# A two-layer transformer step with seven-product multiplications: groups of 8, 8 and 6 feed-forward units, two plain chunk pairs in place of three, and the weight-block sums on GpSimd

## The chip, the core and the metric

One Trainium2 chip; the kernel runs on one of its cores. The metric is the device time of one execution in microseconds (us), the median over runs: 2202.97 us before the change (three runs, 2202.61 to 2203.21). Engines by the names in the profile: PE is TensorE's matmul, PEld its weight load, DVE is VectorE, ACT is ScalarE, POOL is GpSimd, SP starts the DMAs.

## The reference, cut to what matters

Two layers over 640 tokens (128 context, 512 latent) of width 1024. The part of a layer that the change touches is its end, the gated feed-forward with an inner width of 2816 = 22 units of 128, and the projection `h @ w_in` at its start, which is computed by the same routine.

```python
h2 = rmsnorm(x, norm2_g) * (1.0 + sc2) + sh2
a, b = jnp.split(h2 @ w_ffn_in, 2, axis=-1)
return x + g2 * ((jax.nn.silu(a) * b) @ w_ffn_out)
```

All data are float32. The kernel multiplies in a reduced format: each operand is split into a rounded high part and a remainder (low part), and a product is three matmuls: high by high, high by low, low by high.

## The kernel before, in words

**Chunks.** A chunk is 128 output rows by 640 tokens. TensorE reads a weight block of 128x128 and passes 320 tokens, so a plain chunk over a depth of 1024 is 8 x 3 x 2 = 48 matmuls of 320 columns. Chunks come in pairs; in the feed-forward the pair is one unit's `a` and `b`.

**Eight products and seven.** A plain pair is 96 matmuls (in block terms eight half-depth products). A fast pair uses seven half-depth products, P1 to P7 (a Strassen-Winograd scheme), of 12 matmuls each: 84. It needs, of the raw weights of each pair, four sums of blocks of 128x512 (`weight_sums`, numbered 1 to 4, executed in the order 1, 3, 2, 4), and of the activations four blocks of sums and differences per layer and place, made once (`turned_sums`, four of 128x1280, then a high part each by ACT in `turned_hi` and a low part by DVE in `turned_lo`; they are written to `TT` and, for number 1, over part of `H`). Sum 1 is the weight of P5, sum 3 that of P7, sum 2 that of P6, sum 4 that of P3.

**Ring.** The weights of the products, split in high (`fast_hi`, ACT) and low (`fast_lo`, DVE), stand in a ring of six slots inside `wr`. The two halves of the ring are also the two buffers for the weights of plain chunks. `HI_STEP` says after which product a slot is free again. The order of the products is written out by `ring_order`: P1 of pair 0, then for each pair P2, P6, P7, P5, P1 of the next pair, P3, P4. ACT and DVE walk through the same list (`fast_step`): at each step they take results out of PSUM (ACT those of P1, P6, P7 and P3; DVE those of P2, P5 and P4), then split the weights of a product that comes six steps later. Each engine works strictly in the order of its program.

**Banks.** A pair's P1, P6, P5 and P3 accumulate in one bank, `lp[m % 2][:, 0]`; P2 goes to `lp[0][:, 1]`, P7 and P4 to `lp[1][:, 1]`. P6 may start only when ACT has copied P1's result out (`p1_out`), P5 only when ACT has copied P6's (`u2_out`), P3 only when DVE has added P5's (`c22_out`), P4 only when ACT has copied P7's (`p7_out`).

**Groups.** The 22 feed-forward units are computed in three groups, A, B and C (8, 7 and 7). Group A begins with three plain pairs (`first_pair`, then `chunk`), and during these ACT adds the shift to the normalised rows (`raw_rows`) and ACT and DVE make the four turned blocks. Then come the fast pairs (5 in A, 7 in B, 7 in C; 6 at the layer's start, behind three plain pairs), and behind each group its part of the second product (`outward`: 8 chunks over 8, 7 and 7 units), which starts when the last products have left their banks and its weights are split (`out_first_hi`, `weight_lo`). The values that `outward` reads, `G`, are finished pair by pair (`c12_out` by ACT, a multiplication and `hidden_lo` by DVE).

**Sums before.** The four weight sums of a pair are made by DVE between its other work: 2 x 25 pairs x 4.

**Loads.** SP issues the raw weights of a pair in two parts; a slot is free again when the pair two before it has been split. The second part of an odd pair lies in `wx`, over the activations' raw rows, and for the first such load of group A SP waits until turned blocks have been read (`t_lo`).

The lines that decide where the second product's first weights may be written are these, and the change leaves them as they are:

```python
places = [i % RING for i in range(n)]
if places[-1] == 0:
    places[-1] = RING // 2
...
used = max(i for i, r in enumerate(RING_AT[g]) if r // (RING // 2) == s)
act.wait_ge(prod, OPS * pairs_before(l, g, 0) + used + 1)
```

Of the kernel before, what the change touches and what calls it, by code (L numbers as in the profile page):

```python
# [52 lines left out]
FA, FB, FC = 8, 7, 7  # L53
PLAIN = 3
# [4 lines left out]
SLOTS = (2 * PLAIN, N_GATE, KD, 2 * PLAIN, KD, 0, KD, 0, KD)  # L59
SLOT0 = [sum(SLOTS[:i]) for i in range(10)]  # L60
CHUNKS = (2 * PLAIN, 2 * N_GATE, KD, 2 * PLAIN, KD, 0, KD, 0, KD)
# [13 lines left out]
FAST = ((IN_A + IN_B) // 2 - PLAIN, FA - PLAIN, FB, FC)  # L75
FAST0 = [sum(FAST[:i]) for i in range(5)]
FIRST = (PLAIN, PLAIN, FA, FA + FB)
INNER0 = (0, PLAIN, 0, 0)
# [141 lines left out]
def build(nc, xT, ada, adb, win, wgu, wo, wff, wfa, wfb, vec, cond, fgv, cst, rope, dft, bias, ckT, cvt,  # L220
          yT, okT, ovt):
    with ExitStack() as ctx:
# [318 lines left out]
        def _(sy):  # L541
# [24 lines left out]
            def raw_pair(l, g, m):  # L566

                for part in range(2):
# [3 lines left out]
                    else:  # L572
                        before = 1 + l * PER_SLOT + SLOT0[AHEAD[g]] // 2
                        sy.wait_ge(w_lo[0 if r == 0 else 1], before)
                        if r == 3 and g <= FAST_A:
                            sy.wait_ge(t_lo, turned_set(l, g) + 3)
# [42 lines left out]
            for l in range(L):  # L619
# [83 lines left out]
                for j in range(PLAIN):  # L703
                    for s in range(2):
                        weight(l, FF_A, wff, j, s)
                for g in FF_GROUPS:
# [9 lines left out]
                    for s in range(2):  # L716
                        sy.wait_ge(op_lo, nth_op(l, g, FAST[g] - 1, (P3, P4)[s]))
# [32 lines left out]
        def _(pe):  # L750
# [45 lines left out]

            def fill(l, p, place):

                for n, k in FILL.get((p, place), ()):
# [8 lines left out]
                    else:  # L808
                        if k == KD:
# [172 lines left out]
            def fast_product(l, g, i):  # L982
# [26 lines left out]
                if which == P5:  # L1009
                    pe.wait_ge(u2_out, n + 1)  # L1010
                    if new_blocks:
                        pe.wait_ge(t_lo, turned_set(l, g) + 4)
                if which == P3:
                    pe.wait_ge(c22_out, n + 1)
                if which == P4:
                    pe.wait_ge(p7_out, n + 1)
                    if new_blocks:
                        pe.wait_ge(t_lo, turned_set(l, g) + 3)
# [19 lines left out]
            for l in range(L):  # L1038
# [68 lines left out]
                for i, (m, which) in enumerate(ORDER[FAST_IN]):  # L1107
# [6 lines left out]
                    if which == P4:  # L1114
# [18 lines left out]
                for out_of in (c11_out, c12_out, c21_out):  # L1133
                    pe.wait_ge(out_of, pairs_before(l, FAST_IN, FAST[FAST_IN]))
# [49 lines left out]
                for j in range(1, PLAIN):  # L1184
# [4 lines left out]
                for g, inner in zip(FF_GROUPS, (S_GA, S_GB, S_GC)):  # L1189
# [27 lines left out]
        def _(act):  # L1217
# [108 lines left out]

            def fast_step(l, g, i):
# [6 lines left out]
                if which == P1:  # L1334
                    if n:
                        act.wait_ge(c11_out, n)
                    if g == FAST_A and m == 0:
                        act.wait_ge(split, l * PER_SPL + SP0[S_GA] + 2)
                    act.activation(t1[:, 0:TH], A, ACT.Copy).then_inc(p1_out, 1)
# [84 lines left out]
            for l in range(L):  # L1424
# [38 lines left out]
                for o in range(RING // 2, RING):  # L1463
# [76 lines left out]
                def plain_hidden(i, s):  # L1540
# [11 lines left out]
                plain_hidden(0, 0)  # L1552
# [5 lines left out]
                act.wait_ge(lin[1], 1 + l * PER_DR + D0[FF_A] + PLAIN)  # L1558
                turned_hi(l, FAST_A, 1)
                for g in FF_GROUPS:  # L1560
# [4 lines left out]
                    for o in range(RING // 2, RING):  # L1565
# [17 lines left out]
            root(2 * L + 1)  # L1583

        @block.vector
        def _(ve):
# [254 lines left out]
            def weight_sums(l, g, m, which):  # L1841

                if m >= FAST[g]:
                    return
                n = pairs_before(l, g, m)
                a, b = raw(m, 0), raw(m, 1)
                a11, a12, a21, a22 = a[:, 0:QC], a[:, QC:2 * QC], b[:, 0:QC], b[:, QC:2 * QC]
                for s in which:
                    if s == 1:
# [430 lines left out]
```

## Time and profile before

| | |
|---|---|
| median of three runs | 2202.97 us (2202.61 to 2203.21) |
| the profiled execution | 2201.25 us, its span 2199.5 us |
| PE busy | 2137.2 us, 97% of the span |
| DVE busy | 1309.4 us, 60% |
| ACT busy | 900.8 us, 41% |
| POOL busy | 0.2 us, four small writes at the start |

A busy row of PE counts each matmul with its latency, so rows overlap; how long a matmul really takes is read from the start of one merged row to the start of the next. "Idle before" behind a row is the time in which the engine did nothing before it, and the arrow names the instruction that ended it ("issue" where the profile shows none). The chain of waits lies on PE nearly all the time.

### The profile page before, as it was taken

Reading aid. Unit: us, or ns where it says so; the run is one execution under the profiler, and the core shown is the slowest. Engines: PE = TensorE matmul, PEld = TensorE weight load, DVE = VectorE, ACT = ScalarE, POOL = GpSimd, SP = SyncE. Lnnn points to the kernel's source line nnn. Section 1 sums busy time; section 2 is a strip of 40 time slices with the busy share of each in tenths; the row PEclk is TensorE's granted clock in tenths of the full one; section 3 lists DMA queues with packets and bytes.
Section 4 is the critical chain, followed back from the end, with each engine's and each line's share of the span. In section 5 each row is a group of like instructions: output and inputs, shape, how many; then the busy total and the mean of one; then the engine's idle time right before and its main releaser. Section 6 shows DMA issues by size and latency. Waiting matters only on the chain. (4 is left out here: it accounts for less than half of the span.)

```text
span 2199.5 us, 38208 instructions
## 1 busy us (share of the span) xinstructions
PE 2137.2 (97%) x15247; PEld 2012.3 (91%) x15247; DVE 1309.4 (60%) x2493; ACT 900.8 (41%) x1574; POOL 0.2 (0%) x4
## 2 busy tenths in 40 slices
PE   8999999999999999999999999999999999999997
PEld 7998887888998999999989988888899899999997
DVE  5665656665447737558466575566644575484764
ACT  4533443443326415425344344444433363252441
POOL 0000000000000000000000000000000000000000
PEclk9999999999999999999999999999999999999998
DMA  7633321112241422322454233111124132222222
GB/s 294 226 139 105 122 77 49 49 49 67 95 157 63 151 90 90 128 91 77 148 180 171 86 129 120 46 49 49 49 97 155 61 97 68 87 77 77 87 73 82
DMA packets 70774, 225.81 MB, mean 103 GB/s; under 512 B 6992, under 2 KB 13776, under 8 KB 70480
## 3 DMA queue, kind: packets, MB, share of 16 engines
q1 hardware_dynamic: 70608, 223.50, 30.5%
q8 instruction: 116, 1.90, 0.4%
q14 instruction: 50, 0.41, 0.1%
HBM read 215.48 MB, written 6.55 MB: 101 GB/s over the span
## 5 line engine op out<-in xcount | busy, mean ns | idle before, releaser
L755 PE MATMUL lp<-H,wr 128*128 128x320 f32 x4800 | 764.9, 313 | 14.2 <-DVE H L1611 8.0
L755 PEld LDWEIGHTS lp<-H,wr 128*128 128x128 f32 x4800 | 707.4, 188 | 41.5 <-issue 27.2
L1022 PE MATMUL lp<-H,wr 128*128 128x320 f32 x2256 | 350.7, 310 | 5.4 <-DVE tmp L1901 4.0
L1022 PEld LDWEIGHTS lp<-H,wr 128*128 128x128 f32 x2256 | 334.2, 188 | 12.2 <-issue 11.4
L755 PE MATMUL lp<-G,wr 128*128 128x320 f32 x2112 | 311.2, 309 | 3.2 <-issue 3.2
L755 PEld LDWEIGHTS lp<-G,wr 128*128 128x128 f32 x2112 | 309.8, 187 | 5.0 <-issue 5.0
L1239 ACT ACTIVATE wr<-wst 128x1280 fp32r<-128x1280 f32 (+2 forms) x136 | 153.5, 1129 | 179.1 <-PE lp L755 178.5
L1633 DVE TENSOR_TENSOR wr<-wst,wr 128x1280 fp32r<-128x1280 f32 (+2 forms) x152 | 198.3, 1305 | 40.9 <-ACT wr L1239 35.4
L1022 PE MATMUL lp<-TT,wr 128*128 128x320 f32 x1368 | 213.1, 308 | 2.1 <-issue 2.1
L1325 ACT ACTIVATE wr<-wst 128x512 fp32r<-128x512 f32 x256 | 159.6, 627 | 127.5 <-PE lp L1022 75.4
L1022 PEld LDWEIGHTS lp<-TT,wr 128*128 128x128 f32 x1368 | 203.7, 188 | 2.5 <-issue 2.5
L1653 DVE SCALAR_TENSOR_TENSOR x<-lp,mod,x 128x128 f32 (+3 forms) x192 | 72.6, 433 | 195.4 <-PE lp L755 195.4
L1872 DVE TENSOR_TENSOR wr<-wst,wr 128x512 fp32r<-128x512 f32 x256 | 173.4, 684 | 9.1 <-ACT wr L1325 8.9
L755 PE MATMUL lp<-BR,wr 128*128 128x320 f32 x960 | 161.1, 313 | 1.8 <-DVE tmp L1690 1.8
L755 PEld LDWEIGHTS lp<-BR,wr 128*128 128x128 f32 x960 | 143.3, 188 | 7.3 <-issue 3.0
L1281 ACT ACTIVATE prob<-ss,st 128x640 f32<-128x640 f32 (+1 forms) x88 | 59.8, 679 | 132.3 <-DVE st L1732 130.9
L1281 ACT ACTIVATE prob<-sp,st 128x640 f32<-128x640 f32 (+3 forms) x72 | 51.4, 714 | 130.0 <-DVE st L1728 119.1
L1260 ACT ACTIVATE tmp<-lp,vc 128x640 f32<-128x640 f32 x64 | 50.7, 792 | 120.9 <-PE lp L755 120.9
L1293 ACT ACTIVATE pts<-ss 128x640 f32<-128x640 f32 (+3 forms) x120 | 64.3, 571 | 64.5 <-PE ss L923 43.0
L1731 DVE TENSOR_REDUCE st<-ss 128x1 f32<-128x640 f32 (+1 forms) x88 | 59.4, 674 | 50.4 <-PE ss L896 37.8
L1528 ACT ACTIVATE tmp<-x 128x640 f32 (+1 forms) x32 | 23.6, 739 | 153.8 <-DVE x L1653 153.8
L1690 DVE SCALAR_TENSOR_TENSOR tmp<-tmp,lp 128x640 f32<-128x640 f32 x48 | 39.2, 816 | 69.6 <-PE lp L755 69.4
(202 smaller groups left out, 2121.5 us busy)
## 6 DMA issues: line engine op xcount, KB each, us to landing
wst<-wgu SPq DMA_DIRECT2D x64, 640.0 KB, 3.9
wst<-wff SPq DMA_DIRECT2D x72, 512.0 KB, 3.7
sm<-adb SPq DMA_DIRECT2D x13, 2048.0 KB, 8.3
wst<-win SPq DMA_DIRECT2D x30, 512.0 KB, 4.2
wst<-wfb SPq DMA_DIRECT2D x32, 448.0 KB, 3.3
bt<-bias SPq DMA_DIRECT2D x32, 320.0 KB, 3.4
adae<-adb SPq DMA_DIRECT2D x8, 1024.0 KB, 15.2
wst<-wo SPq DMA_DIRECT2D x16, 512.0 KB, 3.7
```

The costliest lines, as they stand in the source:

```text
L755: mm = pe.matmul(out[:, h, 0:TH], w[wi], act[:, ai, k, h * TH:(h + 1) * TH], start=first and i == 0, stop=last and i == 2)
L1022: mm = pe.matmul(bank(m, which), operand(g, i, wi)[:, k * P:(k + 1) * P], passing(g, which, ai, k), start=fresh and k == 0 and j == 0, sto ...
L1239: act.activation(wr[:, s, 0, 0:w], wst[:, s, 0:w], ACT.Copy).then_inc(w_hi[s], 1)
L1260: act.activation(halves(tmp[:, 2 + n % 2, :]), lp[0][:, :, 0:TH], ACT.Tanh, bias=vc[:, i:i + 1], scale=0.5).then_inc(drained[0], 1)
L1281: act.activation(prob[:, u, lo:hi], src, ACT.Exp, bias=nm[:, q:q + 1], scale=SC_DIFF if kind == "df" else 1.0, accum_out=rs[:, q:q + 1]).t ...
L1293: act.activation(pts[:, f % 2, lo:KEYS], sflat[u][:, lo:KEYS], ACT.Copy).then_inc(pt_out, 1)
L1325: act.activation(operand(g, i, 0), source(m, which), ACT.Copy).then_inc(op_hi, 1)
L1633: ve.tensor_tensor(wr[:, s, 1, 0:w], wst[:, s, 0:w], wr[:, s, 0, 0:w].bitcast(F32), ALU.subtract).then_inc(w_lo[s], 1)
L1653: m = ve.scalar_tensor_tensor(out=x[:, k, a:b], in0=lp[s][:, h, a - h * TH:b - h * TH], scalar=mod[:, gate + 2 * j + s, c:c + 1], in1=x[:, ...
L1690: ve.scalar_tensor_tensor(out=halves(mg[:, kd, :] if first else tmp[:, 1, :]), in0=gate, scalar=1.0, in1=up, op0=ALU.add, op1=ALU.mult).th ...
L1731: own.step(ve.tensor_reduce(mx, S[:, at_:at_ + KEYS - lo], AX.X, ALU.max))
L1872: ve.tensor_tensor(operand(g, i, 1), source(m, which), operand(g, i, 0).bitcast(F32), ALU.subtract).then_inc(op_lo, 1)
```

## The change

Six things are changed together.

1. The groups have 8, 8 and 6 units, and group A begins with two plain pairs (`PLAIN_FF`) where it had three. So there are 6, 8 and 6 fast pairs in A, B and C.
2. Where a group has an even number of fast pairs, as all four now have, the last pair computes P4 before P3.
3. `outward` waits for its two banks one after the other (`first_bank_free`, `second_bank_free`) instead of for both at its start.
4. ACT copies the first pair's P1 out (`first_product_out`) before it splits the weights of the fifth and sixth product of the group, not after.
5. In group A the turned blocks are made at other places: number 2 behind the first three weight splits, then 3, 1 and 4; `t_lo` is waited for in that order.
6. The four weight sums of all 52 fast pairs are made by GpSimd.

```diff
-FA, FB, FC = 8, 7, 7
-PLAIN = 3
+FA, FB, FC = 8, 8, 6
+PLAIN, PLAIN_FF = 3, 2
...
-FAST = ((IN_A + IN_B) // 2 - PLAIN, FA - PLAIN, FB, FC)
+FAST = ((IN_A + IN_B) // 2 - PLAIN, FA - PLAIN_FF, FB, FC)
...
-        order += [(m, P3), (m, P4)]
+        order += [(m, P3), (m, P4)] if m + 1 < pairs or pairs % 2 else [(m, P4), (m, P3)]
...
+            def first_bank_free(l, g):
+                other = FAST[g] % 2 == 0
+                pe.wait_ge(c11_out, pairs_before(l, g, FAST[g]))
+                pe.wait_ge(c12_out, pairs_before(l, g, FAST[g] - other))
+            def second_bank_free(l, g):
+                pe.wait_ge(c12_out, pairs_before(l, g, FAST[g]))
+                pe.wait_ge(c21_out, pairs_before(l, g, FAST[g]))
...
-                    if which == P4:
+                    if which == (P3 if m == FAST[FAST_IN] - 1 else P4):
                         turn_chunk(c0)
...
                     def outward(j, ready=None):
                         for s in range(2):
+                            if isinstance(j, int) and j == 0:
+                                (second_bank_free if s else first_bank_free)(l, g)
...
-                    pe.wait_ge(c11_out, pairs_before(l, g, FAST[g]))
-                    pe.wait_ge(c12_out, pairs_before(l, g, FAST[g]))
-                    pe.wait_ge(c21_out, pairs_before(l, g, FAST[g]))
...
                 def plain_hidden(i, s):                       # ACT
...
-                    if i == PLAIN - 1:
+                    if i == PLAIN_FF - 1:
                         for o in range(RING // 2):
                             fast_hi(l, FAST_A, o)
+                        turned_hi(l, FAST_A, 2)
+                        turned_hi(l, FAST_A, 3)
...
-                plain_hidden(1, 1)
-                for which in (2, 3, 4):
-                    turned_hi(l, FAST_A, which)
-                plain_hidden(2, 0)
+                plain_hidden(1, 0)
                 turned_hi(l, FAST_A, 1)
                 for g in FF_GROUPS:
...
-                    for o in range(RING // 2, RING):
+                    fast_hi(l, g, RING // 2)
+                    first_product_out(l, g, 0)
+                    if g == FAST_A:
+                        turned_hi(l, g, 4)
+                    for o in range(RING // 2 + 1, RING):
                         fast_hi(l, g, o)
...
+        @block.gpsimd
+        def _(po):
+            def weight_sums(l, g, m, which):
+                n = pairs_before(l, g, m)
+                a, b = raw(m, 0), raw(m, 1)
+                a11, a12, a21, a22 = a[:, 0:QC], a[:, QC:2 * QC], b[:, 0:QC], b[:, QC:2 * QC]
...
+                    elif s == 2:
+                        po.wait_ge(w_sum, 4 * n + 2)
+                        po.wait_ge(op_lo, nth_op(l, g, m, P1))
+                        po.tensor_tensor(a11, s1t[:], a11, ALU.subtract).then_inc(w_sum, 1)
...
                 def plain_hidden(i, s):                       # DVE
...
                         fast_lo(l, FAST_A, 0)
-                        weight_sums(l, FAST_A, 0, (2,))
                         fast_lo(l, FAST_A, 1)
                         fast_lo(l, FAST_A, 2)
+                        turned_lo(l, FAST_A, 1, 2)
```

The start of group A's fast pairs on ACT, layer 0, before: behind `raw_rows` two plain pairs (L1543, L1550) with the three `TT` blocks between them, then the block written to `H`, the splits of the fourth to sixth product, and P1's copy (L1339).

```order
348 L1543 ACTIVATE tmp<-lp 128x640 [waits lin0]
349 L1239 ACTIVATE wr<-wst 128x1024 [waits lin0,ld_w0]
350 L1239 ACTIVATE wr<-wst 128x1024 [waits lin1,ld_w1]
351 L1550 ACTIVATE G<-tmp 128x640 [waits drained1]
352 L1397 ACTIVATE TT<-mg 128x1280 [waits t_sum] x3
353 L1543 ACTIVATE tmp<-lp 128x640 [waits lin0]
354 L1325 ACTIVATE wr<-wst 128x512 [waits ld_q0,lin0] x2
355 L1325 ACTIVATE wr<-wst 128x512 [waits w_sum,lin0]
356 L1550 ACTIVATE G<-tmp 128x640 [waits drained1]
357 L1397 ACTIVATE H<-mg 128x4x320 [waits t_sum,lin1]
361 L1339 ACTIVATE tmp<-lp 128x320 [waits split,c11_out,prod]
```

The same stretch on ACT now, from the last of `raw_rows` to the copy of P6's result (L1362):

```order
348 L1564 ACTIVATE tmp<-lp 128x640 [waits lin0]
349 L1337 ACTIVATE wr<-wst 128x512 [waits ld_q0,lin0] x2
350 L1337 ACTIVATE wr<-wst 128x512 [waits w_sum,lin0]
351 L1416 ACTIVATE TT<-mg 128x1280 [waits t_sum] x2
352 L1573 ACTIVATE G<-tmp 128x640 [waits drained1]
353 L1416 ACTIVATE H<-mg 128x4x320 [waits t_sum,lin1]
354 L1337 ACTIVATE wr<-wst 128x512 [waits w_sum,lin1]
355 L1347 ACTIVATE tmp<-lp 128x320 [waits split,c11_out,prod]
356 L1416 ACTIVATE TT<-mg 128x1280 [waits t_sum]
357 L1337 ACTIVATE wr<-s1t 128x512 [waits w_sum,lin1]
361 L1384 ACTIVATE tmp<-tmp 128x320 [waits c11_out]
362 L1362 ACTIVATE tmp<-lp 128x320 [waits c21_out,prod]
```

One plain pair is gone from it, and the three splits now stand in front of the `TT` blocks; the third of them (number 350, P6's weight) waits for a sum.

DVE at the same place now, behind the four turned sums (L1969), to P2's result (L1926):

```order
766 L1969 TENSOR_TENSOR mg<-mg 128x4x320 [waits t_sum] x2
767 L1901 TENSOR_TENSOR wr<-wst,wr 128x512 [waits op_hi] x3
768 L1974 TENSOR_TENSOR TT<-mg,TT 128x1280 [waits t_hi]
769 L2132 TENSOR_TENSOR tmp<-lp,tmp 128x640 [waits drained0,lin1]
770 L2137 TENSOR_TENSOR G<-tmp,G 128x640 [waits a_hi,drained1]
771 L1901 TENSOR_TENSOR wr<-wst,wr 128x512 [waits op_hi]
772 L1974 TENSOR_TENSOR TT<-mg,TT 128x1280 [waits t_hi]
773 L1974 TENSOR_TENSOR H<-mg,H 128x4x320 [waits t_hi]
774 L1901 TENSOR_TENSOR wr<-s1t,wr 128x512 [waits op_hi]
775 L1974 TENSOR_TENSOR TT<-mg,TT 128x1280 [waits t_hi]
776 L1901 TENSOR_TENSOR wr<-wst,wr 128x512 [waits op_hi]
777 L1926 TENSOR_TENSOR tmp<-tmp,lp 128x320 [waits prod,p1_out,hid]
```

Before, all four sums and all low parts of the turned blocks but one stood in front of the last plain pair's product; now three of the four low parts stand behind it.

PE at the end of group A in layer 0, before:

```order
535 L1022 MATMUL lp<-TT,wr 128x320 x24
536 L1022 MATMUL lp<-H,wr 128x320 x24
537 L1022 MATMUL lp<-TT,wr 128x320 x12
538 L1033 MATMUL ss<-sm_57,cds 32x256 x8
539 L755 MATMUL lp<-G,wr 128x320 x96
```

And now:

```order
540 L1036 MATMUL lp<-H,wr 128x320 x12
541 L1036 MATMUL lp<-TT,wr 128x320 x12
542 L1047 MATMUL ss<-sm_57,cds 32x256 x8
543 L1036 MATMUL lp<-H,wr 128x320 x12
544 L756 MATMUL lp<-G,wr 128x320 x96
```

P5 and P3 (both on `H`) stood next to each other before; P4 (on `TT`) now stands between them.

## Rows read from the trace of the kernel before

**Rows 1.** The page: span, and busy time by engine.
```profile
span 2199.5 us, 38208 instructions
PE 2137.2 (97%) x15247; PEld 2012.3 (91%) x15247; DVE 1309.4 (60%) x2493; ACT 900.8 (41%) x1574; POOL 0.2 (0%) x4
```

**Rows 2.** Who PE waited for: line, releaser, us in total, times, longest.
```profile
PE lp L1022 <- DVE tmp L1901: 4.0, 6, 0.7
PE lp L755 <- issue: 3.2, 4, 0.8
PE lp L1022 <- issue: 2.1, 2, 1.0
PE lp L1022 <- DVE qk L1901: 1.3, 2, 0.7
```

**Rows 3.** Timeline, end of group C, layer 0: start, us, engine, instructions, idle before.
```profile
1055.19 1.92 PE L1022 MATMUL lp<-H,wr 128*128 128x320 f32 x12
1057.79 2.00 PE L1022 MATMUL lp<-H,wr 128*128 128x320 f32 x12 [0.67 <-DVE tmp L1901]
1059.62 1.92 PE L1022 MATMUL lp<-TT,wr 128*128 128x320 f32 x12
1062.35 49.51 PE L755 MATMUL lp<-G,wr 128*128 128x320 f32 x336 [0.80 <-issue]
```

**Rows 4.** Timeline, plain pairs of group A, layer 0.
```profile
678.16 7.01 PE L755 MATMUL lp<-H,wr 128*128 128x320 f32 x46 [0.43 <-DVE wr L1633]
686.77 0.68 ACT L1543 ACTIVATE tmp<-lp 128x640 f32<-128x640 f32 x1
686.90 4.54 DVE L1946 TENSOR_TENSOR mg<-mg 128x1280 f32<-128x1280 f32 x3 [2.13 <-ACT mg L1389]
691.36 1.22 DVE L1633 TENSOR_TENSOR wr<-wst,wr 128x1024 fp32r<-128x1024 f32 x1
692.63 14.08 PEld L755 LDWEIGHTS lp<-H,wr 128*128 128x128 f32 x96 [0.39 <-DVE wr L1633]
694.20 3.58 ACT L1397 ACTIVATE TT<-mg 128x1280 fp32r<-128x1280 f32 x3
```

**Rows 5.** Timeline, start of the fast pairs of group A, layer 0.
```profile
707.02 0.82 DVE L2112 TENSOR_TENSOR tmp<-lp,tmp 128x640 f32<-128x640 f32 x1 [2.85 <-PE lp L755]
707.88 0.74 ACT L1550 ACTIVATE G<-tmp 128x640 fp32r<-128x640 f32 x1 [4.43 <-DVE tmp L2112]
708.53 1.26 ACT L1397 ACTIVATE H<-mg 128x1280 fp32r<-128x1280 f32 x1
709.69 0.61 ACT L1325 ACTIVATE wr<-wst 128x512 fp32r<-128x512 f32 x1
709.82 1.49 DVE L1951 TENSOR_TENSOR H<-mg,H 128x1280 fp32r<-128x1280 f32 x1 [0.27 <-ACT H L1397]
711.25 0.41 ACT L1339 ACTIVATE tmp<-lp 128x320 f32<-128x320 f32 x1
711.76 3.76 PE L1022 MATMUL lp<-TT,wr 128*128 128x320 f32 x24 [1.03 <-issue]
713.63 0.48 DVE L1897 TENSOR_TENSOR tmp<-tmp,lp 128x320 f32<-128x320 f32 x1
```

**Rows 6.** DVE's groups by line, one of the sums: count, busy us, mean ns.
```profile
L1862 DVE TENSOR_TENSOR wst<-s1t,wst 128x512 f32<-128x512 f32 x50 | 34.6, 692 | 2.0
```

**Rows 7.** Timeline, second weight buffer at the end of group A, layer 0.
```profile
777.30 1.05 ACT L1377 ACTIVATE wr<-wst 128x1024 fp32r<-128x1024 f32 x1
778.38 1.23 DVE L1633 TENSOR_TENSOR wr<-wst,wr 128x1024 fp32r<-128x1024 f32 x1
```

**Rows 8.** Stretches between the layers: us, busy by engine, granted clock, DMA.
```profile
1113.00:1114.00 1.00, 1.00 (x18) 0.41 (x10) 0.03 (x1) 0.94 (x2) 0.00 (x0) 1.00 0.20 77
1115.00:1116.00 1.00, 1.00 (x14) 0.53 (x17) 1.00 (x2) 0.27 (x1) 0.00 (x0) 0.51 0.69 225
1117.00:1118.00 1.00, 1.00 (x5) 0.86 (x5) 0.00 (x0) 0.00 (x0) 0.00 (x0) 0.50 0.85 184
```

More of the change, by code:

```diff
@@ L702, in _ @@
                 outward_weights(W_O, wo, 3)
-                for j in range(PLAIN):
+                for j in range(PLAIN_FF):
                     for s in range(2):
@@ L715, in _ @@
                     src = (wfa, wfb[:, :, :, 0:FB * P], wfb[:, :, :, FB * P:(FB + FC) * P])[g - FAST_A]
-                    for s in range(2):
-                        sy.wait_ge(op_lo, nth_op(l, g, FAST[g] - 1, (P3, P4)[s]))
+                    last = FAST[g] - 1
+                    for s, freed in enumerate(((last - 1, P4), (last, P3)) if last % 2 else ((last, P3), (last, P4))):
+                        sy.wait_ge(op_lo, nth_op(l, g, *freed))
                         weight(l, out, src, 0, s)
@@ L1011, in fast_product @@
                     if new_blocks:
-                        pe.wait_ge(t_lo, turned_set(l, g) + 4)
+                        pe.wait_ge(t_lo, turned_set(l, g) + (3 if g == FAST_A else 4))
                 if which == P3:
@@ L1017, in fast_product @@
                     if new_blocks:
-                        pe.wait_ge(t_lo, turned_set(l, g) + 3)
+                        pe.wait_ge(t_lo, turned_set(l, g) + (4 if g == FAST_A else 3))
                 fresh = which in (P1, P2, P7)
@@ L1132, in _ @@
                     mm.then_inc(f1, 1)
[L1133 to L1134 removed]
+                first_bank_free(l, FAST_IN)
                 fill(l, 0, "f")
@@ L1183, in _ @@
                 first_pair(l, FF_A, S_H2)
-                for j in range(1, PLAIN):
+                for j in range(1, PLAIN_FF):
                     for s in range(2):
@@ L1325, in fast_hi, with first_product_out @@
                 act.activation(operand(g, i, 0), source(m, which), ACT.Copy).then_inc(op_hi, 1)
+            def first_product_out(l, g, m):
+                n = pairs_before(l, g, m)
+                act.wait_ge(prod, OPS * pairs_before(l, g, 0) + PLACE[g][m, P1] + 1)
+                if n:
+                    act.wait_ge(c11_out, n)
+                if g == FAST_A and m == 0:
+                    act.wait_ge(split, l * PER_SPL + SP0[S_GA] + PLAIN_FF - 1)
+                act.activation(tmp[:, 1, 0:TH], bank(m, P1), ACT.Copy).then_inc(p1_out, 1)
             def fast_step(l, g, i):
@@ L1334, in fast_step @@
                 if which == P1:
[L1335 to L1339, printed above, removed]
+                    if m:
+                        first_product_out(l, g, m)
                 if which == P6:
@@ L1564, in _ @@
                             fast_hi(l, g, o)
-                    for o in range(RING // 2, RING):
+                    fast_hi(l, g, RING // 2)
+                    first_product_out(l, g, 0)
+                    if g == FAST_A:
+                        turned_hi(l, g, 4)
+                    for o in range(RING // 2 + 1, RING):
                         fast_hi(l, g, o)
@@ L1583, in _ @@
             root(2 * L + 1)
+        @block.gpsimd
+        def _(po):
+            def weight_sums(l, g, m, which):
+                n = pairs_before(l, g, m)
+                a, b = raw(m, 0), raw(m, 1)
+                a11, a12, a21, a22 = a[:, 0:QC], a[:, QC:2 * QC], b[:, 0:QC], b[:, QC:2 * QC]
+                for s in which:
+                    if s == 1:
+                        for part in range(2):
+                            po.wait_ge(ld_q[2 * (m % 2) + part], 16 * slot_uses(l, g, m))
+                        if n:
+                            before = (l, g, m - 1) if m else (l, g - 1, FAST[g - 1] - 1) if g else (l - 1, FAST_C, FAST[FAST_C] - 1)
+                            po.wait_ge(op_lo, nth_op(*before, P5))
+                        po.tensor_tensor(s1t[:], a21, a22, ALU.add).then_inc(w_sum, 1)
+                    elif s == 3:
+                        po.wait_ge(w_sum, 4 * n + 1)
+                        po.tensor_tensor(a21, a11, a21, ALU.subtract).then_inc(w_sum, 1)
+                    elif s == 2:
+                        po.wait_ge(w_sum, 4 * n + 2)
+                        po.wait_ge(op_lo, nth_op(l, g, m, P1))
+                        po.tensor_tensor(a11, s1t[:], a11, ALU.subtract).then_inc(w_sum, 1)
+                    else:
+                        po.wait_ge(w_sum, 4 * n + 3)
+                        po.wait_ge(op_lo, nth_op(l, g, m, P2))
+                        po.tensor_tensor(a12, a12, a11, ALU.subtract).then_inc(w_sum, 1)
+            for l in range(L):
+                for g in range(4):
+                    for m in range(FAST[g]):
+                        weight_sums(l, g, m, (1, 3, 2, 4))
         @block.vector
```

70 lines of the change are left out of this document (19 added, 51 removed).

## The prediction, made before the change was run

> **What bounds the kernel now.** I read the page first, then the list of who PE waited for, then the timeline at the ends of the groups and at the start of group A, each time start to start. PE is busy for 97% of the span, DVE for 60%, ACT for 41%, and GpSimd has nothing to do [rows 1]. So the time falls only where PE has fewer matmuls or shorter waits, and it rises where PE has to wait anew; DVE time that is freed is worth nothing unless PE waits for DVE there. Inside the fast pairs PE waits for DVE before each group's last P3, six times in the feed-forward and twice at the layer's start, four times at the start of the second product, and twice at the start of group A [rows 2]. All other steps of the fast pairs run without a gap, so the 200 sums that DVE makes now are hidden. That also caps what the change can win in these stages.
>
> The unit of the sum is a matmul of 320 columns: 336 of them in 49.51 us [rows 3], 0.1474 us; a product of 12 takes 1.77 us.
>
> **Part 1, fewer matmuls (item 1).** One pair a layer goes from 96 matmuls to 84: 24 x 0.1474 = 3.5 us less. With the third plain pair goes its wait for split weights. The second pair starts at 678.16, so it is through 96 x 0.1474 = 14.15 us later, at 692.31; the third starts at 692.63 [rows 4]: 0.32 us, 0.6 us in two layers. Moving units from B and C to A and B leaves the second product at 22 x 8 chunk units, the same matmuls.
>
> **Part 2, P4 before the last P3 (item 2).** Before, P5 starts at 1055.19 and P3 at 1057.79 [rows 3], 2.60 us for a product of 1.77: 0.83 us lost because DVE must add P5 first. With P4 in between DVE has 1.77 us for what takes 0.83. Six times in the feed-forward: 5.0 us less. At the layer's start the same wait [rows 2] goes, but the transposes behind the last product then wait for ACT's copy of P3, which before was covered by P4; I count 0.2 us less for both layers together.
>
> **Part 3, the second product starts on a free bank (item 3).** P4 starts at 1059.62, the second product at 1062.35 [rows 3]: 2.73 us for 1.77, 0.95 lost. Four groups show it [rows 2]; in the other two a small adaLN product covers it. With an even number of pairs the last pair lies in the other bank, so the wait goes, for group A of layer 1 and group C of both: 3 x 0.95 = 2.8, less 0.1 for A, where splitting 1024 columns on DVE (1.23 [rows 7]) now comes behind the adding of P4 (0.48 [rows 5]): 2.7 us.
>
> Group B does not win. With 8 pairs there are 56 products; the ring place of the last two, number 54 and 55, is 54 mod 6 = 0 and 55 mod 6 = 1, and the rule that moves a last product out of the first half looks only at one whose place is 0. With 7 pairs (49 products) that rule held, and with 6 pairs the last six stand in order. So in group B the first half of the ring, which is the first buffer of the second product's weights, is read until the very last product ends. ACT's split and then DVE's come behind it: 1.05 + 1.23 [rows 7], 0.2 for the handovers and 0.15 for the drain of the last matmul, 2.6 us. Layer 0 loses 2.6 where it lost nothing, layer 1 2.6 - 0.95: 4.25 us more.
>
> **Part 4, sums on GpSimd inside the groups (item 6).** 208 sums leave DVE, and no PE wait in the middle of a group goes with them. On GpSimd they hang on loads and on DVE's low parts, much earlier than they are needed. A pair has 12.4 us of PE time; four sums fit as long as one, d, is below 3.1 us. No row shows d. GpSimd is here not faster than DVE at its own operation, 0.69 us [rows 6]; for the upper end I take DVE's time for two and a half times the columns, 1.49 [rows 5]. I calculate with 1.49: a two-input operation in software is nearer to the slow end than to DVE's own pace, and d enters the sum only once a layer (part 5). The Trainium skill (GPSIMD Engine Reference, Performance versus the Vector engine) gives 4497 ns for 2048 columns; a quarter, 1.1 us, is an estimate, and by it the total below would be 0.7 us lower. No run here shows it yet.
>
> **Part 5, the start of group A (items 1, 4, 5).** Here the change takes 14.1 us of PE time away from under ACT's and DVE's preparations. Times are of layer 0; layer 1 has the same pattern. DVE ends the turned sums at 686.90 + 4.54 = 691.44 [rows 4], whatever else changes, since they wait for ACT's rows. PE ends the second plain pair at 692.3, then a small transposition, P1 from 692.6 and P2 to 696.1. P6 must wait for ACT's copy of P1, and in ACT's program that copy now stands behind: P6's weight, which needs sum 2, which needs DVE's low part of P1; the two `TT` blocks; the high part of `G`, which waits for DVE's multiplication; the block in `H`; and P7's weight. The chain from 691.36 on (an operation queued behind another starts 0.08 us before its end [rows 4], about what the handovers cost): low part 0.69, sum d, split 0.61, one block 3.58 / 3 = 1.19 [rows 4], its low part 1.49, multiplication 0.82, `G` 0.74, block in `H` 1.26, split 0.61, copy 0.41 [rows 5]: 7.8 + d, so P6 starts at 699.2 + d. **First hole: 3.1 + d.** Then P6 and P7 run to 702.75 + d. P5 needs ACT's copy of P6, which stands behind ACT's Silu on P2's result, and DVE adds P2 (0.48) only after it has made low parts of P7's weight, of three blocks and of two more weights: from 698.8 + d on 0.69 + 1.49 + 1.49 + 0.69 + 1.49 + 0.69 + 0.48, less six times 0.08, then two ACT operations of 0.41: P5 at 706.2 + d. **Second hole: 3.45.** The raw weights of pair 1 come late too (SP waits for the fourth block), but I find them in time for its P6. Before, this place cost 1.03 [rows 2] plus 0.15 of drain, 1.2. So a layer loses 3.1 + 1.49 + 3.45 - 1.2 = 6.85, both 13.7 us; with d = 0.69 it is 12.1. The first item that item 4 gains, ACT's copy ahead of two splits, is inside this chain; in B and C there was no wait for it.
>
> **Sum.** Less: 3.5 + 0.6 + 5.0 + 0.2 + 2.7 = 12.0. More: 4.25 + 13.7 = 17.95. Net +5.9 us on the profiled execution's 2201.25, which lies 1.7 us under the median; on the median 2202.97 + 5.9 = 2208.9 us. With d = 0.69 it is +4.3.
>
> **Rivals.**
> - *The second hole does not open, or neither does (other side).* For it: the cap on the gain is real, and P4, P3 and bank waits surely go. Against it: every step of the chain is in ACT's or DVE's program order. Without the second hole the net is 5.9 - 6.9 = -1.0, 2202.0 us. If the two holes together stay at what was there before, 1.2 a layer, it is 4.25 - 12.0 = -7.75: 2195.2 us. It decides at (12.0 - 4.25) / 2 + 1.2 = 5.1 us of holes a layer; above that the kernel is slower.
> - *GpSimd and DVE hold each other up.* A GpSimd sum and a DVE operation that reads two tensors of SBUF would not run side by side. In group A's start sum 3 then sits in front of the second turned sum (0.4), sum 2 behind the low part of P2 (0.69), and P6's low part behind sum 4 (0.4): 1.5 us a layer, 3.0 us in all, 2211.9 us. In the middle of the groups DVE's free time covers it. For it nothing in the trace, since GpSimd is idle there. The Trainium skill (SBUF — State Buffer, SBUF: two separate sides) says that the shared port pair is an exclusive lock for a whole instruction, also against a DVE operation with two SBUF inputs; no run here shows that yet.
> - *The clock falls in the holes.* Between the layers the granted clock goes from 1.00 to 0.50, 2.4 to 1.2 GHz, and stays there for about 3 us [rows 8], after a stretch of short matmuls. If it falls in the first hole, P6 and P7 run slower while P5 waits anyway. If it falls in the second, 3 us at half clock cost 1.5 us a layer: 2211.9 us.
> - *GpSimd is too slow.* With d above 3.1 us the sums set the pace; at 4 us, 52 x 3.6 = 187 us more. Nothing in the trace excludes it, but the operation is a plain one.
>
> **How the numbers follow.** Forecast as summed 0.47; held up by each other 0.20; clock 0.08; no second hole 0.12; no new hole 0.10; GpSimd too slow 0.03. The range goes from 2201.5, just under the case without a second hole, to 2215.5, where holding up and clock come together with d at its upper end; left out are the case without holes, the very slow GpSimd and a little at the ends, 0.18. By itself the forecast's range is 2206 to 2211. What a measurement can tell from no change is 0.2%, 4.4 us. Faster by more: 0.10. Within: 0.12 and the low end of the forecast, 0.06, 0.18. Slower: the rest, 0.72.
>
> **What would show it.** In the profile after: 24 fewer matmuls; no wait of about 0.67 before the last P3 of a feed-forward group; no wait at the second product of A and C, and about 2.5 us at that of B in both layers, ended by DVE's weight split; at group A's start two waits of PE, about 4.6 us before P6 ended by ACT's copy, and about 3.4 before P5. GpSimd's sums give d. The prediction is wrong if these two waits are short, if PE waits in the middle of a group for sums, or if DVE's operations of 0.69 us are longer while GpSimd works.

## The result, and the profile after

The changed kernel takes 2223.3 us (median of 4 runs, 2222.5 to 2224.4) beside 2203.1 for the kernel before: the ratio is 1.009, interval 1.0078 to 1.0102. It is 20.2 us slower. The forecast was 2208.9, in a range up to 2215.5: the direction was right, the size less than a third of what came (5.9 us).

Rows of the page after, against [rows 1]: 24 matmuls fewer, GpSimd busy, and PE busy for longer although it has less to do. Such a PE is a slower PE: the mean granted clock of the profiled run is 0.986, before it was 0.996.

```profile
span 2222.6 us, 38240 instructions
PE 2148.8 (97%) x15223; PEld 2023.3 (91%) x15223; DVE 1261.2 (57%) x2309; ACT 902.3 (41%) x1592; POOL 305.9 (14%) x212
```

Who PE waited for, against [rows 2] (the lines have moved: 1022 is 1036 now, 755 is 756). The wait before the last P3 of a group has gone, the "issue" waits at the start of the fast pairs too. New are 4.9 us before P6 at the start of group A and, not forecast, 2.3 and 2.5 us for ACT's line 1362, which is the copy of P6's result that P5 needs.

```profile
PE lp L1036 <- ACT tmp L1347: 9.8, 2, 4.9
PE lp L756 <- issue: 5.6, 3, 2.8
PE lp L1036 <- ACT tmp L1362: 4.8, 2, 2.5
```

The end of group C in layer 0, against [rows 3]: P5, P4, P3 and the second product follow each other in 1.76, 1.76 and 1.84 us. Both waits that parts 2 and 3 were to remove are gone.

```profile
1075.74 1.92 PE L1036 MATMUL lp<-H,wr 128*128 128x320 f32 x12
1077.50 1.92 PE L1036 MATMUL lp<-TT,wr 128*128 128x320 f32 x12
1079.26 1.92 PE L1036 MATMUL lp<-H,wr 128*128 128x320 f32 x12
1081.10 42.47 PE L756 MATMUL lp<-G,wr 128*128 128x320 f32 x288
```

The end of group B, the P3 and the second product, first of layer 0 and then the start of layer 1's: the waits that the ring was to cause, 2.64 and 2.81 us idle, in layer 0 2.9 us start to start (4.67 less a product of 1.77), against 2.6 forecast from [rows 7]. In layer 1 the product then also starts at a lower clock.

```profile
945.82 2.03 PE L1036 MATMUL lp<-H,wr 128*128 128x320 f32 x12
950.49 56.56 PE L756 MATMUL lp<-G,wr 128*128 128x320 f32 x384 [2.64 <-issue]
2033.72 26.56 PE L756 MATMUL lp<-G,wr 128*128 128x320 f32 x169 [2.81 <-issue]
```

The start of group A's fast pairs in layer 0 on PE, against [rows 5]: P1 and P2, P6 and P7 behind the first hole, then P5 with two more products, and from 720.86 on the second pair's P6, P7 and P5. Two groups take longer than such groups do elsewhere: 24 matmuls 6.30 us (3.68 at 720.86), 36 matmuls 7.05 (5.44 further on).

```profile
696.22 3.79 PE L1036 MATMUL lp<-H,wr 128*128 128x320 f32 x24
704.94 6.30 PE L1036 MATMUL lp<-TT,wr 128*128 128x320 f32 x24 [4.93 <-ACT tmp L1347]
711.98 5.53 PE L1036 MATMUL lp<-H,wr 128*128 128x320 f32 x36 [0.74 <-DVE wr L1901]
720.86 3.68 PE L1036 MATMUL lp<-TT,wr 128*128 128x320 f32 x24
726.86 7.05 PE L1036 MATMUL lp<-H,wr 128*128 128x320 f32 x36 [2.33 <-ACT tmp L1362]
```

Stretches with the granted clock (the third number from the right), after, against [rows 8]: it is between its two levels of 1.2 and 2.4 GHz on average behind the first hole, and at the lower one (half clock from here on) at the start of the attention; there it was 1.00 in the trace before.

```profile
704.00:712.00 8.00, 6.32 (x25) 6.12 (x25) 7.45 (x9) 5.00 (x10) 0.00 (x0) 0.59 0.07 22
200.00:204.00 4.00, 4.00 (x18) 3.73 (x17) 3.49 (x11) 0.84 (x4) 0.00 (x0) 0.50 0.00 0
```

Sums on GpSimd and low parts on DVE, against [rows 6]; a low part took 684 ns on average before.

```profile
L1630 POOL TENSOR_TENSOR wst<-s1t,wst 128x512 f32<-128x512 f32 x52 | 84.0, 1616 | 42.1 <-DVE wr L1901 41.4
L1626 POOL TENSOR_TENSOR wst<-wst 128x512 f32<-128x512 f32 x26 | 34.2, 1316 | 2.0
L1901 DVE TENSOR_TENSOR wr<-wst,wr 128x512 fp32r<-128x512 f32 x260 | 237.7, 930 | 45.5 <-ACT wr L1337 45.5
```

**Where the time lies.** Start to start in the two traces; the forecast is for both layers together, the traces for layer 0 and layer 1:

| stretch | forecast, both layers | traces |
|---|---|---|
| first plain pair of A to A's second product | +7.1 | +8.3 and +7.9 |
| A's second product to the layer's end | -0.95 | -0.2 and +0.85 |
| all else (layer's start, attention, W_O, normalization) | -0.2 | +7.0, both layers |

Together +23.9, of which 0.8 is given back at the very end. The two profiled runs lie 1.8 under and 1.0 over the medians of their kernels, so that 20.2 is left of 23.1. Three things are to be explained: 9 us too much at the start of A, 1.6 behind it, and 7 in all else, where the change moves sums and, at the layer's start, P4, P3 and the copy of P1. By the medians the third is smaller: 20.2 less the first two rows, 16.9 here and 18.0 in the second profile of the same kernel (E5 below), leaves 2 to 3 us.

### The profile page after: what moved, and what is told of

Its sections match the earlier page's. It is cut to its first block and busy times, and to the rows that moved or that the text cites. A ratio compares the mean times of both kernels' runs of the same rounds, so it can differ in the third digit from the quotient of the medians.

```text
span 2222.6 us, 38240 instructions
## 1 busy us (share of the span) xinstructions
PE 2148.8 (97%) x15223; PEld 2023.3 (91%) x15223; DVE 1261.2 (57%) x2309; ACT 902.3 (41%) x1592; POOL 305.9 (14%) x212
## 5 line engine op out<-in xcount | busy, mean ns | idle before, releaser
L1901 DVE TENSOR_TENSOR wr<-wst,wr 128x512 fp32r<-128x512 f32 x260 | 237.7, 930 | 45.5 <-ACT wr L1337 45.5
L1623 POOL TENSOR_TENSOR s1t<-wst 128x512 f32<-128x512 f32 x26 | 36.5, 1405 | 1567.7 <-DMA wst<-wff 1338.0
L1036 PE MATMUL lp<-TT,wr 128*128 128x320 f32 x1440 | 229.4, 313 | 9.8 <-ACT tmp L1347 9.8
L1036 PEld LDWEIGHTS lp<-TT,wr 128*128 128x128 f32 x1440 | 219.5, 192 | 10.2 <-issue 10.2
L1251 ACT ACTIVATE wr<-wst 128x1024 fp32r<-128x1024 f32 (+2 forms) x132 | 149.2, 1131 | 180.6 <-PE lp L756 180.2
L1689 DVE TENSOR_TENSOR wr<-wst,wr 128x1024 fp32r<-128x1024 f32 (+2 forms) x148 | 193.4, 1307 | 43.3 <-ACT wr L1251 35.0
L1634 POOL TENSOR_TENSOR wst<-wst 128x512 f32<-128x512 f32 x52 | 79.6, 1531 | 103.1 <-DVE wr L1901 102.4
L1630 POOL TENSOR_TENSOR wst<-s1t,wst 128x512 f32<-128x512 f32 x52 | 84.0, 1616 | 42.1 <-DVE wr L1901 41.4
```

The lines of the kernel that those rows point to most:

```text
L1036: mm = pe.matmul(bank(m, which), operand(g, i, wi)[:, k * P:(k + 1) * P], passing(g, which, ai, k), start=fresh and k == 0 and j == 0, sto ...
L1251: act.activation(wr[:, s, 0, 0:w], wst[:, s, 0:w], ACT.Copy).then_inc(w_hi[s], 1)
L1630: po.tensor_tensor(a11, s1t[:], a11, ALU.subtract).then_inc(w_sum, 1)
L1634: po.tensor_tensor(a12, a12, a11, ALU.subtract).then_inc(w_sum, 1)
L1689: ve.tensor_tensor(wr[:, s, 1, 0:w], wst[:, s, 0:w], wr[:, s, 0, 0:w].bitcast(F32), ALU.subtract).then_inc(w_lo[s], 1)
L1901: ve.tensor_tensor(operand(g, i, 1), source(m, which), operand(g, i, 0).bitcast(F32), ALU.subtract).then_inc(op_lo, 1)
```

## The experiments

Theory G: GpSimd's sums hold DVE up, and so PE. Theory S (later L): the start of A with two plain pairs is to blame, its late raw weights above all. Theory C: much of it is half clock that comes and goes.

**E5, the changed kernel again.** No edit.

> The changed kernel once more, beside the kernels of this group. Theory C (some of its 20 us is half clock outside the feed-forward that the same kernel has in one run and not in another): 2216 to 2221 here, with a mean granted clock of 0.988 to 0.991, and the difference to its first profile lies at the start of the attention and in the normalizations. If nothing of it is chance: 2222 to 2225, clock 0.986 to 0.988.

2223.3 us (2221.2 to 2224.7), ratio 1.0088 (1.0073 to 1.0104), clock 0.986 to 0.989. So the total is no chance, and theory C's 2216 to 2221 fails. Its places move, though: the attention's start lost 0.64 and 1.12 us here, 1.70 and 1.01 in the first profile.

**E1, E3, E2: sums and start apart.** E1 is the kernel before with `weight_sums` moved to GpSimd's program (200 sums in it, not the 208 of the expectation); E3 the changed kernel with `PLAIN_FF = 3` and the start of A in the old order; E2 the changed kernel with

```
-        @block.gpsimd
...
-                        weight_sums(l, g, m, (1, 3, 2, 4))
...
+                if which == P2:
+                    weight_sums(l, g, m + 1, (1,))
+                if which == P6:
+                    weight_sums(l, g, m + 1, (3, 2))
...
+                if which == P1 and m:
+                    weight_sums(l, g, m, (4,))
...
```

> The kernel before (groups 8/7/7, three plain pairs, order and waits unchanged), only its 208 weight sums moved from DVE to GpSimd. Before is 2203.1 us, after 2223.3. Theory G (GpSimd holds DVE up, and most of the 14 us that my sum lacked follow from that): the DVE low parts are near 0.9 us here too, and the kernel is slower than before by 5 to 9 us, 2208 to 2212, with PE waits on DVE or ACT that before doesn't have and the granted clock at 0.50 at the start of the attention. Theory S (the start of group A with two plain pairs does it all; the sums are hidden wherever they are made): 2202 to 2204. Theory C (the clock falls where the stages happen to lie in time): 2203 to 2206, without new waits.

2203.3 beside 2204.0 us: ratio 0.9997 (0.9987 to 1.0006). The low parts take 922 ns here too, yet nothing is lost but 0.4 and 0.8 us at the layers' starts, where PE waits for DVE's copies of the values. Theory G alone is refuted: the lengthened DVE operations cost nothing where DVE has time to spare.

> The changed kernel (8/8/6, sums on GpSimd, its order and bank waits), but group A starts as in the kernel before: three plain pairs, five by fast products, turned blocks in the old places. By the trace the start of A costs 8.3 and 7.9 us a layer net of what it saves; without it, and without a gain in A, 2207. Theory S: 2206 to 2208, or less if the half clock outside the feed-forward goes too (2201). Theory G: GpSimd goes on costing in the second pair of A and at the layer's start, 2209 to 2213.

2204.4, ratio 1.0005 (0.9995 to 1.0015), under theory G's 2209 to 2213 and between the 2206 to 2208 and the 2201 of theory S. Against the changed kernel's 1.009 the start of A is worth some 18 us; by the traces its stretch is 8.7 and 8.8 us shorter than in the changed kernel.

> The changed kernel, only its weight sums made by DVE again, at the places where the kernel before makes them (for the first pair of group A two behind the first turned sum and one behind each of two low parts). Theory G: the second pair's P5 in group A no longer waits (2.33 us and 1.6 us of half clock behind it, per layer), the first hole shortens by 1 us, the 2 us at the layer's start and some 5 us of half clock outside the feed-forward go: 2208 to 2211. Theory S: only the sum in the first hole shortens (1.6 to 0.7 us, twice) and the raw weights of the second pair stay late: 2219 to 2222. Theory C: 2211 to 2216.

2216.5, ratio 1.0061 (1.0043 to 1.0079): some 6 us less, between theories G and S and just above what theory C gave (2211 to 2216). PE at the start of A, layer 0: the first hole is 3.60 instead of 4.93, the wait before the second pair's P5 is gone, but P3 of the first pair now waits 1.64 us.

```profile
699.59 6.28 PE L1036 MATMUL lp<-TT,wr 128*128 128x320 f32 x24 [3.60 <-ACT tmp L1347]
707.23 3.76 PE L1036 MATMUL lp<-H,wr 128*128 128x320 f32 x24 [1.36 <-DVE wr L1896]
712.63 2.00 PE L1036 MATMUL lp<-H,wr 128*128 128x320 f32 x12 [1.64 <-DVE tmp L1925]
```

DVE at that place: it stands 1.96 us before the second pair's first sum, whose raw weights (`wx`) have not landed, and what P3 waits for is queued behind.

```profile
708.86 0.69 DVE L1879 TENSOR_TENSOR s1t<-wx 128x512 f32<-128x512 f32 x1 [1.96 <-issue]
712.00 0.48 DVE L1925 TENSOR_TENSOR tmp<-tmp,lp 128x320 f32<-128x320 f32 x1
```

**E6, the third pair's sums held back.**

```
+                        if g == FAST_A and m == 2:
+                            po.wait_ge(c11_out, n)
                         po.tensor_tensor(s1t[:], a21, a22, ALU.add).then_inc(w_sum, 1)
```

> The changed kernel with one more wait: in group A GpSimd starts the third pair's sums only when DVE has added the second pair's P2. In the trace two DVE operations ahead of that addition took 1.70 and 1.91 us while GpSimd made those sums (0.69 and 0.82 elsewhere), and behind the addition stand ACT's Silu and the copy for which P5 of the second pair waits 2.33 us. Theory G (held up by GpSimd): both are short again, the wait falls to 0.2 to 0.5 us, the half clock behind it (1.6 us) goes, 3 to 3.6 us a layer, 6 to 7 us under the changed kernel. Rival S (the second pair's raw weights come too late): the wait stays within 0.3 us, same time, or later by up to 2 us.

First the changed kernel: DVE, then GpSimd, ahead of the wait of 2.33 us.

```profile
721.21 1.70 DVE L1901 TENSOR_TENSOR wr<-wst,wr 128x512 fp32r<-128x512 f32 x1
722.84 1.91 DVE L1952 TENSOR_TENSOR tmp<-tmp 128x640 f32<-128x640 f32 x1
724.78 0.49 DVE L1926 TENSOR_TENSOR tmp<-tmp,lp 128x320 f32<-128x320 f32 x1
```

```profile
721.06 1.30 POOL L1623 TENSOR_TENSOR s1t<-wst 128x512 f32<-128x512 f32 x1 [1.92 <-DVE wr L1901]
722.44 1.62 POOL L1626 TENSOR_TENSOR wst<-wst 128x512 f32<-128x512 f32 x1
724.14 1.73 POOL L1630 TENSOR_TENSOR wst<-s1t,wst 128x512 f32<-128x512 f32 x1
```

With the added wait, DVE and then PE at the same place:

```profile
721.57 0.68 DVE L1903 TENSOR_TENSOR wr<-wst,wr 128x512 fp32r<-128x512 f32 x1
722.17 0.81 DVE L1954 TENSOR_TENSOR tmp<-tmp 128x640 f32<-128x640 f32 x1
723.02 0.49 DVE L1928 TENSOR_TENSOR tmp<-tmp,lp 128x320 f32<-128x320 f32 x1
```

```profile
725.11 5.69 PE L1036 MATMUL lp<-H,wr 128*128 128x320 f32 x36 [0.41 <-ACT tmp L1362]
738.50 5.52 PE L1036 MATMUL lp<-H,wr 128*128 128x320 f32 x36 [0.66 <-ACT tmp L1362]
```

1.70 and 1.91 become 0.68 and 0.81, the wait 0.41, the 36 matmuls 5.69: as theory G had it, and rival S, no move, falls. But the sums then meet DVE later: in layer 0 one pair on (0.66 at 738.50), in layer 1 before P3 of the second pair (1.04 us, behind three DVE operations of 1.77 to 1.91). The kernel gains 3.2 us, 2220.1, ratio 1.0079 (1.0064 to 1.0095), not 6 to 7. That interval overlaps the changed kernel's (1.0073 to 1.0104), so the total alone doesn't show a gain; the start of A does, 2.1 and 2.5 us shorter in the trace. The Trainium skill (SBUF — State Buffer, SBUF: two separate sides) calls the port pair that GpSimd shares with DVE an exclusive lock for a whole instruction, for a DVE operation with two SBUF inputs. The trace agrees: the two that read SBUF twice are held, the addition that reads PSUM takes 0.49 us beside a sum of GpSimd's.

**E11 and E12, the second pair's weights early.** The load of its second part went to `wx`, which the turned blocks use; SP issued it at 710.12, behind the last block's low part. In both runs the load goes to two buffers, `wxa` and `wxb`, with no such wait.

```
-                        if r == 3 and g <= FAST_A:
-                            sy.wait_ge(t_lo, turned_set(l, g) + (4 if g == FAST_A else 3))
+                        if r == 3 and g == FAST_A:
+                            for half, t, done in ((0, wxa, ld_q[r]), (1, wxb, ld_e)):
...
```

> The changed kernel, only the second part of the second pair's raw weights in group A is loaded into two buffers of its own, so that the load needn't wait for the last turned block (in the trace it was issued at 710.12 and GpSimd's first sum of that pair began at 713.71). Theory L (the late load is the root: it makes the second pair's sums, splits and low parts late, and DVE's backlog then meets GpSimd's next sums): the second pair's sums begin behind 708.7, 5 us earlier, the wait of 2.33 before its P5 falls under 0.5 and the half clock behind it goes: 3 to 4 us a layer, 2215 to 2217 beside the changed kernel's 2223. Theory G (GpSimd meets DVE there whenever the load comes): the wait stays over 1.5 us, 2220 to 2223.

2219.0, ratio 1.0080 (1.0063 to 1.0097). The second pair's P5 waits 0 and 0.20 us: theory L holds for that wait. But its sums, now early, meet DVE in the first pair. GpSimd, DVE, and PE:

```profile
705.39 2.37 POOL L1640 TENSOR_TENSOR s1t<-wxa,wxb 128x512 f32<-128x512 f32 x1 [9.51 <-DVE wr L1918]
707.84 1.59 POOL L1643 TENSOR_TENSOR wxa<-wst,wxa 128x512 f32<-128x512 f32 x1
```

```profile
706.54 1.77 DVE L1918 TENSOR_TENSOR wr<-wst,wr 128x512 fp32r<-128x512 f32 x1
708.63 3.64 DVE L1918 TENSOR_TENSOR wr<-wst,wr 128x512 fp32r<-128x512 f32 x3
```

```profile
709.63 8.32 PE L1049 MATMUL lp<-H,wr 128*128 128x320 f32 x36 [2.52 <-issue]
```

P5 of the first pair comes 8.12 us behind its P6 (7.04 in the changed kernel), and the 36 matmuls take 8.32, at a granted clock of 0.62 and 0.52 in the 8 us from 708 on. So in layer 0 nothing is won: the stretch to A's second product is 122.4 us in both kernels. In layer 1 it is 2.7 us shorter. The total is between the two theories, and its interval overlaps the changed kernel's.

> The same early load with the weight sums on DVE. With the sums on DVE and the late load (2216.5), DVE stood 1.96 us before the second pair's first sum and PE waited 1.64 and 1.79 us for DVE's addition of P5. Theory L: both waits go, 3.5 us less, 2212 to 2214. If DVE's own sums are the cause: 0 to 1 us less, 2215 to 2217.

2211.4, ratio 1.0043 (1.0026 to 1.0060): with the sums on DVE both waits go, P3 and the second pair run through.

```profile
703.39 5.22 PE L1049 MATMUL lp<-TT,wr 128*128 128x320 f32 x24 [3.61 <-ACT tmp L1362]
711.03 5.52 PE L1049 MATMUL lp<-H,wr 128*128 128x320 f32 x36 [2.42 <-DVE wr L1913]
```

Its stretch from the first plain pair to A's second product is 3.5 and 3.0 us longer than before. My sum gives 3.15 and 2.3 for it, with d = 0.69. The agreement is not of every step, since here DVE makes the sums itself: P5 starts 7.64 us behind P6, where the sum has 7.0.

**E8, PE kept busy.**

```
+                for _ in range({(0, P6): 28, (0, P5): 18, (1, P5): 14}.get((m, which), 0) if g == FAST_A else 0):
+                    pe.matmul(ss[0][:, 0, 0:TH], H[:, 0, 0, 0:P], H[:, 0, 0, 0:TH], start=True, stop=True)
```

> The changed kernel with 60 matmuls of 320 columns a layer whose result nobody reads, put before PE's waits at the start of group A: 28 before P6 of the first pair (4.1 us in a wait of 4.9), 18 before its P5 (2.7 us) and 14 before P5 of the second pair (2.1 us in a wait of 2.4). It asks what the half clock there costs. If PE's own activity decides the clock: P6 with P7 takes 3.7 us instead of 6.2, but P5 starts where it did, since it waits for DVE and ACT (nothing gained there); the three products behind the second pair's P5 take 5.4 instead of 7.05 us, 1.6 us less a layer: 3 us less in all, 2220 beside 2223. If the clock falls for another reason: same durations, 2223. If P5 follows P6 and P7, not DVE: 2.5 us a layer more, 2215.

```profile
701.69 3.84 PE L1038 MATMUL lp<-TT,wr 128*128 128x320 f32 x24 [0.73 <-issue]
708.73 5.52 PE L1038 MATMUL lp<-H,wr 128*128 128x320 f32 x36 [0.56 <-DVE wr L1903]
723.76 5.52 PE L1038 MATMUL lp<-H,wr 128*128 128x320 f32 x36 [0.43 <-ACT tmp L1364]
```

The granted clock stays at 1.00 from 701 to 730. P6 and P7 take 3.84 us, yet P5 starts 7.04 us behind P6, to the digit as before: half clock in this hole costs nothing. Behind the second pair's P5 it costs 1.5 us. That would make 3 us; the stretch to A's second product is 0.9 and 1.3 us shorter. The run gave 5, 2218.1, ratio 1.0062 (1.0045 to 1.0079), and the rest lies outside of A, where the edit changes nothing.

**E9, P1's copy ahead.** `first_product_out(l, FAST_A, 0)` stands in front of the two `turned_hi` on ACT.

> The changed kernel, only ACT's copy of the first pair's P1 in group A, for which P6 waits 4.9 us, put ahead of the two turned blocks on ACT: it comes 5.8 us earlier. My reading (both holes are one chain on DVE: low parts of P6's weight, three blocks and two more weights, then the addition of P2): P6 starts some 3 us earlier, PE waits before P7 and P5 instead, P5 starts where it did or 0.3 us later; 2222 to 2224. Rival (the queue on ACT is the price of the start): the 3.3 us are won, 2216 to 2218.

```profile
700.38 2.82 PE L1036 MATMUL lp<-TT,wr 128*128 128x320 f32 x12 [1.80 <-DVE TT L1976]
705.69 3.54 PE L1036 MATMUL lp<-TT,wr 128*128 128x320 f32 x12 [2.49 <-DVE TT L1976]
710.88 7.34 PE L1036 MATMUL lp<-H,wr 128*128 128x320 f32 x36 [1.65 <-DVE wr L1903]
```

P6 starts 3 us earlier against P1, and P5 0.3 us later (16.08 us behind P1, 15.76 before): the two holes are one chain on DVE, as I read it. The time, 2219.8, ratio 1.0074 (1.0058 to 1.0091), is lower than I expected, though its interval overlaps the changed kernel's; the second pair's P5 waits 0.61 and 1.00 us here, where it waited 2.33 and 2.49.

**E4, the ring of B.**

```
+    if places[-2:] == [0, 1]:
+        places[-2:] = [3, 4]
```

> The changed kernel, only the last two products of a group of 8 pairs moved from ring places 0 and 1 to 3 and 4, so that the first half of the ring is free two products sooner. All theories: the wait of 2.64 and 2.81 us at the outward product of B goes to under 0.3, and with it the half clock behind the one of layer 1 (1.5 us): 2223.3 - 5.0 - 1.5 = 2217 (2216 to 2219). If it moves less than 4 us, something else was late there too.

```profile
942.61 2.03 PE L1038 MATMUL lp<-H,wr 128*128 128x320 f32 x12
944.48 56.48 PE L758 MATMUL lp<-G,wr 128*128 128x320 f32 x384
```

2213.1, ratio 1.0044 (1.0028 to 1.0061). By the trace 2.8 and 2.6 us of waits and 1.5 of half clock are gone, 7; the other 3 lie outside of B, where the edit changes nothing.

**E7 and E10, the best version.** E3 with the ring of E4, sums on DVE, and P3 ahead of P4 again at the layer's start; E10 is the same with the sums on GpSimd.

> What the experiments point to: the changed kernel's order (P4 ahead of the last P3) and bank waits in the feed-forward, groups of 8, 8 and 6, but three plain pairs and the start of group A as before, sums on DVE, the last two products of B in ring places 3 and 4, and the layer's start as before. By my sum's terms: P4 ahead in B and C 4 x 0.83 = 3.3 us less, the free bank 0.95 each for A of layer 1, B of layer 1 and C of both, 3.8 less: 7.1 under the kernel before, 2196 to 2197 beside 2203 to 2204. If the gains of these terms are not real (the range of the changed kernel with three plain pairs on GpSimd was that of before): 2202 to 2204.

2193.7 (2192.7 to 2196.9), ratio 0.9961 (0.9948 to 0.9975): 9.4 us faster than the kernel before (5.5 to 11.5), where the terms gave 7.1. In the traces its feed-forward, from the first plain pair to the layer's end, is 6.6 us shorter in both layers together.

> The best version so far (2193.7: three plain pairs, 8/8/6, P4 ahead of P3 and bank waits in the feed-forward, ring of B mended), with its weight sums on GpSimd. If GpSimd costs only where DVE has no time to spare: 0.4 and 0.8 us at the layers' starts more, and up to 1 us in the second pair of A, 2194.5 to 2197. If what DVE is spared is worth something: under 2193. If GpSimd holds DVE up on PE's path in every group: 2199 or more.

2196.8, ratio 0.9972 (0.9959 to 0.9985). Its profile loses 0.9 us to E7's at the start of layer 1 and 0.4 in layer 0, as expected; the two intervals overlap. No gain is seen from what DVE is spared, as PE does not wait for it.

## Why the prediction was wrong

**Parts 1 to 3 held.** 24 matmuls fewer, no wait before the last P3, none at C's second product, 2.9 us start to start at B's (forecast 2.6). E7, which has the gains of parts 2 and 3 without the losses, is 9.4 us below the kernel before; their sum, 7.1, lies inside its interval. At the layer's start, though, GpSimd's sums cost 1.2 us (E1), more than the 0.2 won there.

**Part 5 held up to the first P5.** d is 1.3 alone and 1.6 beside DVE (I took 1.49); P6 starts 8.7 us behind P1 (forecast 8.1), after 4.9 us of idle PE, and P5 starts 7.04 us behind P6 where I had 7.0. The 0.6 us is sum 2, 0.1 longer, and the turned sums: their last three took 5.07 us (4.54 in [rows 4]), while GpSimd made sum 3.

```profile
689.87 1.30 POOL L1626 TENSOR_TENSOR wst<-wst 128x512 f32<-128x512 f32 x1
690.50 5.07 DVE L1969 TENSOR_TENSOR mg<-mg 128x1280 f32<-128x1280 f32 x3 [2.14 <-ACT mg L1408]
```

That the second hole hardly shows as a wait is the half clock, in which P6 and P7 fill it.

**The step that failed** is the last of part 5, "The raw weights of pair 1 come late too [...], but I find them in time for its P6", and with it two sentences: part 4's, that inside the groups the sums come much earlier than they are needed, and the second rival's, that DVE's free time covers them there. P6 of the second pair was in time. I stopped there and did not follow what the late load does to DVE behind it. The weights landed at 713.7, the sums ran until 719.1, ACT's split waited for them, and DVE's low parts, bunched up from 718.5 on, met the third pair's sums: 2.1 us of holding up in the two operations before the addition whose Silu and copy P5 waits for. SP's load, GpSimd's first sum, ACT's split and DVE's first low part:

```profile
710.12 0.33 SPq L577 DMA_DIRECT2D wx<-wff  x1
713.71 1.30 POOL L1623 TENSOR_TENSOR s1t<-wx 128x512 f32<-128x512 f32 x1 [14.41 <-DMA wx<-wff]
717.86 0.63 ACT L1337 ACTIVATE wr<-wst 128x512 fp32r<-128x512 f32 x1 [5.13 <-POOL wst L1630]
718.52 1.17 DVE L1901 TENSOR_TENSOR wr<-wst,wr 128x512 fp32r<-128x512 f32 x1 [4.01 <-ACT wr L1337]
```

That is 2.33 us and 1.6 of half clock behind it in layer 0, much the same in layer 1: 8 of the 9 us, and the first hole's 0.6 and 0.5 are the rest. E6 takes the meeting away and the wait falls to 0.41 and 0.25; E11 takes the late load away and the wait falls to 0 and 0.20, but DVE is held up in the first pair; E12 takes both away, and the stretch comes within 0.4 and 0.8 us of my sum. I had GpSimd and DVE holding each other up as a rival at 3.0 us, in the first pair. There it made 0.5 and 0.3 us; the larger part came in the second pair, where I had put it at nothing.

**The clock** was a rival, put at 1.5 us a layer behind the second hole alone. Rows show half clock behind three waits: the first hole, where it costs the changed kernel nothing (E8), the second pair's P5, 1.6 us a layer, and B's second product, 1.5 us in one of the two layers. Of the 7 us elsewhere, GpSimd's sums at the layers' starts are 1.2; some 5 are half clock at the attention's start and in the normalizations, whose program the change did not alter. The kernel before has such losses too, one of them in [rows 8]: its 44 runs beside the experiments go from 2199.7 to 2207.2 us, the quickest at a mean clock of 0.996, the slowest at 0.992, and its profiled run is near the quickest. How much of the 5 us belongs to the change and how much to the run stays open. Against the profile of the kernel before, E8's loses 3 us at these places and E7's 1 at most; if the start of A and what follows it take in every run what the traces show, the medians leave only 1 to 2 us of the 5.

## What to carry to other kernels

When work is taken from under a preparation, follow the chain beyond the first product that is late: the next buffer's load, what queues behind it, and whom that meets. Here the sums on a second engine cost nothing inside the groups while DVE had time to spare (E1). Where DVE was late, nearly all of the 2.1 us by which they held it up reached PE (1.9 us, E6), and moving them moved the place of the loss. A hole's price was the wait that ended last plus the half clock behind it, not the slow matmuls within it (E8).

## What the runs showed of the hardware

- GpSimd's subtraction of two 128x512 fp32 blocks takes 1.30 us alone and mostly 1.6 to 1.75 beside DVE operations that read two SBUF tensors (one addition 2.37, in E11); these go from 0.69 to 1.70 and from 0.82 to 1.91.
- 256 low parts of 922 instead of 684 ns, some 60 us of DVE time, changed nothing in E1: the mean of an operation says little without its place.
- With sixty matmuls a layer whose result nobody reads, put into PE's waits, the granted clock stayed at 1.00 there and the start of A was 0.9 and 1.3 us shorter (E8). The kernel was 5 us quicker; the rest lies where the edit changes nothing.
